# Routed experts in blocks of 32 slots on four column tiles, with down one block behind and ten shared weight places

## What is computed

```python
grp = argmax(xt @ w_rg + b_rg)                      # 4 groups
top_val, top_idx = top_k(in_grp, 2)                 # 2 of the 8 experts of the group
gate = grp_p[:, None] * softmax(top_val)
expert = grp[:, None] * 8 + top_idx                 # 32 experts
# for every token of an expert e:
hid = silu(xb @ w_gate[e]) * (xb @ w_up[e])         # 1024 -> 512
y = hid @ w_down[e]                                 # 512 -> 1024
out[token] += y * gate
```

## Time and profile before

| | |
|---|---|
| median of 3 runs | 2683.63 us |
| the profiled execution's own time | 2685.92 us |
| its span, from the first to the last instruction | 2684.0 us |
| granted TensorE clock, mean | 0.962 |
| first X to last weighing in `experts_stage` | 467.8 to 1079 us |
| bytes moved by DMA | 451.88 MB |
| read from and written to DRAM | 371.86 MB, 58.94 MB |

### The profile page before, as it was taken

One profiled execution on the slowest core, in us unless ns is written; L12 is line 12 of the kernel. 1 busy time (PEld: TensorE's weight loads), 2 busy tenths in 40 slices (PEclk: granted clock), 3 DMA queues, 4 the chain that ended last, 5 costly groups with the idle time before them and its releaser, 6 DMA issues. The chain is left out here.

```text
span 2684.0 us, 39067 instructions
## 1 busy us (share of the span) xinstructions
PE 2437.0 (91%) x14919; PEld 1265.9 (47%) x14919; DVE 1617.9 (60%) x2819; ACT 1082.1 (40%) x1789; POOL 631.3 (24%) x652
## 2 busy tenths in 40 slices
PE   4999895998899999489999999798999999999999
PEld 3555544554455555245434444344454444444544
DVE  7787776222222232557397999844765756747863
ACT  6111454121112122555455648712553634724820
POOL 2012020000000000232244532100630711703602
PEclk8999897999999999789899999899999999999999
DMA  8785758899999999420001329653002002011133
GB/s 246 194 288 170 237 165 283 316 383 387 387 391 366 387 348 332 140 78 32 24 32 56 110 83 184 128 210 126 9 1 102 9 1 102 9 71 40 64 118 126
DMA packets 207372, 451.88 MB, mean 168 GB/s; under 512 B 103600, under 2 KB 113200, under 8 KB 198768
## 3 DMA queue, kind: packets, MB, share of 16 engines
q1 hardware_dynamic: 171344, 368.02, 39.6%
q10 hardware_dynamic: 25696, 48.93, 5.1%
q0 software_dynamic: 10176, 32.78, 4.2%
HBM read 371.86 MB, written 58.94 MB: 161 GB/s over the span
## 5 line engine op out<-in xcount | busy, mean ns | idle before, releaser
L1490 PE MATMUL m_gu<-conv_y,m_xT 128*64 128x256 f32 x1024 | 232.9, 387 | 18.5 <-DMA arena<-in_moe_w_up 16.2
L2728 POOL TENSOR_TENSOR group_words<-group_words 128x1024 f16<-128x1024 f16 x64 | 153.0, 2412 | 377.5 <-PE i_pj L144 368.3
L1492 PE MATMUL m_gu<-arena,m_xT 128*64 128x256 f32 x1024 | 232.9, 387 | 0.0
L1597 DVE TENSOR_TENSOR m_hid<-m_sg,m_gu 64x256 f32<-64x256 f32 x96 | 39.5, 413 | 318.4 <-ACT m_sg L1541 318.4
L1541 ACT ACT_TABLE_LOAD x48 | 61.6, 1283 | 298.1 <-issue 298.1
L1492 PEld LDWEIGHTS m_gu<-arena,m_xT 128*64 128x64 f32 x1024 | 142.7, 140 | 73.8 <-issue 15.4
L1512 PE MATMUL m_y_ps<-arena,m_hidT 128*64 128x512 f32 x768 | 175.4, 598 | 0.0
L1490 PEld LDWEIGHTS m_gu<-conv_y,m_xT 128*64 128x64 f32 x1024 | 142.8, 140 | 36.3 <-issue 25.3
L142 PE MATMUL i_pj<-hT,group_words 128*128 128x512 f16 x384 | 146.5, 381 | 13.1 <-ACT group_words L352 7.7
L142 PE MATMUL s_pj<-hT,arena 128*128 128x512 f16 x368 | 141.9, 386 | 14.1 <-issue 14.0
L143 PE MATMUL i_pj<-hT,group_words 128*128 128x512 f16 x384 | 146.5, 382 | 0.0
(11 more groups left out here) (629 smaller groups left out, 6462.5 us busy)
## 6 DMA issues: line engine op xcount, KB each, us to landing
arena<-in_moe_w_down SPq DMA_DIRECT2D x32, 2048.0 KB, 24.9
conv_y<-in_moe_w_gate SPq DMA_DIRECT2D x22, 2048.0 KB, 17.1
arena<-in_moe_w_up SPq DMA_DIRECT2D x22, 2048.0 KB, 23.9
hT<-in_moe_w_gate SPq DMA_DIRECT2D x10, 2048.0 KB, 16.2
hT<-in_moe_w_up SPq DMA_DIRECT2D x10, 2048.0 KB, 21.9
x_tok<-in_ada_w ACTq DMA_DIRECT2D x8, 2048.0 KB, 12.1
slot_out<-m_y ACTq DMA_DIRECT2D x96, 128.0 KB, 8.0
arena<-in_w_gates SPq DMA_DIRECT2D x23, 512.0 KB, 3.9
```

The lines of the kernel that those rows point to most:

```text
L1490: g = nc.tensor.matmul(gu_ps[i][g_rows, 0:FFN // 2], lhsT=xT[:, c, :], rhs=k.wg[e % WEIGHT_SLOTS][:, c, cols], start=c == 0, stop=c == KC - 1)
L1492: u = nc.tensor.matmul(gu_ps[i][u_rows, 0:FFN // 2], lhsT=xT[:, c, :], rhs=k.wu[e % WEIGHT_SLOTS][:, c, cols], start=c == 0, stop=c == KC - 1)
L1597: nc.vector.tensor_tensor(hid[:, i, :], sg[:, i, :], gu_ps[i][u_rows, 0:FFN // 2], ALU.mult) \
L2728: return tuple(k.nc.gpsimd.tensor_tensor(k.y_U[:, t % 2, n], k.adt_parts[:, n, t, heads].unsqueeze(2).to_broadcast([P, HPG, P]), k.upto16. ...
```

## The change

Blocks have 32 slots instead of 64 and an expert has at least two. The table says for each of 128 partitions which quarter of which token's row it takes: partition 32j+r holds quarter j (256 values, 1 KB) of the row in slot r. With the counts above there are 88 blocks. X is then 2 transposes of 128x128. GU, Y and the table's matmuls use four column tiles of 32 (`tile(j)`): up columns in tiles 0 and 1, gate columns in tiles 2 and 3, and for Y a quarter of the output in each. Each GU tile takes the columns of its weights in neighbouring pairs, with two columns between pairs left to the other tile. Down is loaded as four neighbouring rows a partition. On PE the order becomes X(n+1), GU(n), Y(n-1), H(n). The gain and the shift are one DVE instruction each. The weights have ten places instead of nine (the tenth is half of `x_tok`), shared by all kinds in turn. Gathers go through a ring of four buffers and a POOL copy; stores move from ACT's queue to POOL's, also through a ring of four.

```diff
-BLOCK = P // 2
-SLOT_BLOCKS = 2 * S // BLOCK + EXPERTS
-TABLE_ROWS = SLOT_BLOCKS + 1
+BLOCK, QUARTER = P // 4, D // 4
+RING = 4
+LEAST = 2
+SLOT_BLOCKS = 2 * S // BLOCK + LEAST * EXPERTS
+TABLE_ROWS = SLOT_BLOCKS + 3 * RING
-ZERO_PARTS = 4
+ZERO_PARTS = 6
...
+    spare = k.x_tok[:, TT // 2:TT, :].rearrange("p t d -> p (t d)")
+    k.places = [arena_units(k, n) for n in range(6)] + [halves_of_hT(k, n) for n in range(2)] + [arena_units(k, 6), spare]
...
+def load_unit(k, eng, i):
+    e, part = i // 3, i % 3
+    name = ("moe_w_gate", "moe_w_up", "moe_w_down")[part]
+    source = k.ins[name][turn_of(e)]
+    eng.dma_start(expert_unit(k, e, part), source.rearrange("(p c) n -> p c n", p=P)).then_inc(k.unit_in[i % PLACES], 16)
...
             for n in range(2):
                 for t in range(TT):
-                    last = nc.tensor.matmul(tab_ps[:, :], lhsT=low_hot[:, n, t, :], rhs=blk_hot[:, n, t, :],
...
+                    for j in range(4):
+                        last = nc.tensor.matmul(tab_ps[j * BLOCK:(j + 1) * BLOCK, :], lhsT=low_hot[:, n, t, :],
...
+            def free(i):
+                sp.wait_ge(y_done if i % 3 == 2 else gu_done, 4 * end(sp, i // 3))
+            for i in range(PLACES, UNITS):
+                if (i - PLACES) % 3 != 1:
+                    free(i - PLACES)
+                load_unit(k, sp, i)
...
+            def hand_on(i, n, before):
+                pool.wait_ge(x_in[i], 4 * n - 4 * i + 16)
+                pool.wait_ge(xt_done, before)
+                nc.gpsimd.tensor_copy(xg[:, :], ring[:, i, :]).then_inc(x_copied, 1)
+                pool.wait_ge(x_copied, n + 1)
+                fetch(i, n + RING)
+            def store(i, n):
+                pool.wait_ge(y_read, n + 2)
+                pool.dma_start(k.slot_out[bass.ds(n * BLOCK, BLOCK), :].rearrange("r (j c) -> j r c", j=4),
+                               y[:, i, :]).then_inc(y_stored[i], 16)
+            def give(i, landed):
+                pool.wait_ge(y_stored[i], landed)
+                pool.sem_inc(y_free, 1)
...
+                for c in range(KC):
+                    for j, (part, i) in enumerate(((1, 0), (1, 1), (0, 0), (0, 1))):
+                        last = nc.tensor.matmul(gu_ps[tile(j), 0:FFN // 2], lhsT=xT[:, c % 2, c // 2, :],
+                                                rhs=half_of(expert_unit(k, e, part)[:, c, :], i), start=c == 0, stop=c == KC - 1)
...
                 for c in range(FC):
+                    for j in range(4):
+                        last = nc.tensor.matmul(y_ps[tile(j), 0:QUARTER], lhsT=hidT[:, c, :],
+                                                rhs=expert_unit(k, e, 2)[:, c % 2 * 2 + c // 2, j * QUARTER:(j + 1) * QUARTER],
...
-                with pe.Fori(first, behind) as n:
-                    GU(n, e)
-                    H(n, 0)
-                    X(n + 1)
-                    H(n, 1)
-                    Y(n, e)
+                X(first + 1)
+                wait_unit(k, pe, e, 0)
+                wait_unit(k, pe, e, 1)
+                GU(first, e)
+                if e:
+                    Y(first - 1, e - 1)
+                H(first)
+                with pe.Fori(first + 1, behind) as n:
+                    X(n + 1)
+                    GU(n, e)
+                    Y(n - 1, e)
+                    H(n)
...
+            with dve.Fori(1, blocks) as n:
+                gained(n + 1)
+                dve.wait_ge(gu_done, 4 * n + 4)
+                shifted(n + 1)
+                product_of(n)
+                weigh(n - 1, (n + RING - 1) & (RING - 1))
```

More of the change, by code:

```diff
@@ L1240, in _ @@
             act.wait_ge(gate_mm, 1)
-            for half in range(2):
-                rows_of = slice(half * BLOCK, (half + 1) * BLOCK)
-                nc.scalar.copy(k.gate_half[rows_of, :], gate_ps[rows_of, half * HALF:(half + 1) * HALF])
+            for j in range(4):
+                rows_of = slice(j * BLOCK, (j + 1) * BLOCK)
+                nc.scalar.copy(k.gate_half[rows_of, 0:QUARTER], gate_ps[rows_of, j * QUARTER:(j + 1) * QUARTER])
         @block.vector
@@ L1361, in alloc_expert_weights, with expert_unit, wait_unit @@
 def alloc_expert_weights(k):
[L1363 to L1385, removed]
+    spare = k.x_tok[:, TT // 2:TT, :].rearrange("p t d -> p (t d)")
+    k.places = [arena_units(k, n) for n in range(6)] + [halves_of_hT(k, n) for n in range(2)] + [arena_units(k, 6), spare]
+    k.unit_in = [k.nc.alloc_semaphore(f"m_unit_in{n}") for n in range(PLACES)]
+def expert_unit(k, e, part):
+    n = FFN if part < 2 else D
+    return k.places[(3 * e + part) % PLACES].rearrange("p (c n) -> p c n", n=n)
+def load_unit(k, eng, i):
[3 more added lines that the diff above has]
+    eng.dma_start(expert_unit(k, e, part), source.rearrange("(p c) n -> p c n", p=P)).then_inc(k.unit_in[i % PLACES], 16)
+def wait_unit(k, eng, e, part):
+    i = 3 * e + part
+    eng.wait_ge(k.unit_in[i % PLACES], 16 * (i // PLACES + 1))
 def experts_stage(k):
@@ L1458, in _, with fetch @@
             blocks = end(pool, EXPERTS - 1)
-            def fetch(n, column):
-                nc.gpsimd.tensor_copy(idx[:, :], column).then_inc(idx_ready, 1)
+            rounds = (blocks + RING) >> 2
+            quarters = k.normed_dram.rearrange("s (j d) -> (s j) d", j=4)
+            def fetch(i, n):
+                column = k.slot_token[:, n:n + 1] if isinstance(n, int) else k.slot_token[:, bass.ds(n, 1)]
+                nc.gpsimd.tensor_copy(idx[:, i:i + 1], column).then_inc(idx_ready, 1)
                 pool.wait_ge(idx_ready, n + 1)
@@ L1471, in _ @@
-            with pool.Fori(1, blocks + 1) as n:
-                pool.wait_ge(xt_done, n)
-                fetch(n, k.slot_token[:, bass.ds(n, 1)])
+            for i in range(RING):
+                fetch(i, i)
+            pool.sem_inc(y_free, RING)
+            for i in range(RING):
+                hand_on(i, i, i + 1)
+            for i in range(RING):
+                hand_on(i, RING + i, RING + i + 1)
+                if i >= 2:
+                    give(i - 2, 16)
+                store(i, i)
@@ new lines, in _ @@
+            with pool.Fori(2, rounds) as g:
+                for i in range(RING):
+                    n = g * RING + i
+                    hand_on(i, n, (n <= blocks) * n + (n > blocks) * (blocks + 1) + 1)
+                    give((i + 2) % RING, g * 16 - 16 + 16 * (i // 2))
+                    store(i, n - RING)
+            for i in range(2, RING):
+                give(i, (blocks >> 2) * 16)
+            for i in range(RING):
+                store(i, (blocks >> 2) * RING + i)
+            for i in range(RING):
+                pool.wait_ge(x_in[i], rounds * 16 + 16)
@@ L1967, in _ @@
                     fetch0(t + 6)
+            for i in range(RING):
+                pool.wait_ge(k.y_stored[i], ((blocks + RING) >> 2) * 16)
         @block.vector
@@ L3416, in mixer_program @@
         k.att_stored = nc.alloc_semaphore("att_stored")
[L3417 removed]
+        k.x_natural, k.normed_stored = [nc.alloc_semaphore(f"x_natural{n}") for n in range(2)], [nc.alloc_semaphore(f"normed_stored{n}") for n in range(4)]
         with ExitStack() as first:
```

228 lines of the change are left out of this document (118 added, 110 removed).

## The result

The changed kernel takes 2692.45 us (median of 8 runs, 2687.04 to 2695.17) against 2681.28 us (8 runs) for the kernel before on the same chip: ratio 1.0039, 95% interval 1.0026 to 1.0051. It is slower by 0.4%, where 1.2% faster was forecast. The profiled execution took 2691.96 us, its span is 2690.3 us.

What follows compares the result with a forecast made beforehand. DMA, at 565 us against PE's 504, was to become the expert stage's bound. The stage's end, -38.5 us, and +7 around it gave -31.5 and a forecast of 2652 us, range 2618 to 2700 (8 in 10).

Steps and rivals of the forecast that it cites:

- rival A: GU and Y on PE: only two tiles work at once, a block takes 10.9 us, about 3040 us; chance 0.11.
- PE's block, 5.73 us: PE, one block: GU 3.44, Y 1.72, X, H and tile changes together 0.57 us; 88 blocks are 504 us.
- Rival B: GU's moving operand: column pairs halve the rate, a block takes 9.2 us, time about 2895 us; chance 0.04.
- The ring puts them four blocks (23 us) ahead: POOL's stream: `hand_on` and gather stand behind a `give` waiting for a store, but run four blocks, 23 us, ahead.
- DMA's sum, 565 us: DMA in the expert stage: weights 487 - 5, `x_tok` reload 5.5, gathers and stores 78 us; becomes the bound.
- the 52 ns: Gathers and stores: each 1 KB run takes 52 ns, on a line between 35 ns (512 bytes) and 87 (2 KB).
- rival D: 1 KB runs at 87 ns add 53 us, about 2705; or POOL with its queue exceeds 5.73 us a block; chance 0.06.
- The stage's end, -38.5 us: Expert stage: the last weighing comes at 1040.5 us, against 1078.3 + 0.7 before.
- Around it, +7: Outside the block loop: router +1.4 and +1, first gathers +2.5, next stage's gathers +2, zeroing 0; sum +7 us.
- the stages outside the experts move by more than 7 us: Sign that the forecast is wrong: stages other than the experts shift by over 7 us.
- PE waits for POOL's copies: Sign that the forecast is wrong: PE waits for POOL's copies or for H instead of for weights.
- Rival C: PE issue: record pairs start 0.063 us apart, not 0.054; a block takes 6.6 us, about 2684, no change; chance 0.1.

Runs made afterwards that it cites:

- e6: Changed kernel with down weights back in 4096-byte packets, and gate, up and hidden columns read as neighbours: 2658.04 us.
- e10: Changed kernel with only the down weights back in 4096-byte packets, column pairs kept: 2673.48 us.
- e15: Changed kernel with 4096-byte down packets, neighbouring columns, and stores on ScalarE's queue as four plain transfers a block: 2646.56 us.
- e5: Changed kernel without the four dummy stores and the last two waits for landed stores behind the loop: 2683.91 us.
- e1: Changed kernel with each block's single store issued from ScalarE one block behind, VectorE waiting for landings, no dummy stores: 2749.37 us.
- e16: Changed kernel with its 16384-byte packets and column pairs kept, stores on ScalarE's queue as four plain transfers a block: 2674.57 us.
- e3: Changed kernel with gate's and up's moving operand read as 256 neighbouring columns instead of column pairs: 2689.19 us.
- e2: Kernel before with down as four neighbouring rows a partition, gate and up on column pairs, hidden columns turned to match: 2702.74 us.

## Why the prediction was wrong

- **Four tiles together** (rival A): right; four records within 0.01 us, twice those of the earlier trace rows. The Trainium skill (TensorE: Matmul & The Clock Gate, Part 3: Packing small matmuls) has matmuls in strict order by start and end; a fourth matmul's first record before the first one's second speaks against that, if the two records of one float32 matmul are neighbours in the order.
- **PE's block, 5.73 us**: mis-sized; measured 6.26. H and X together take 0.74 us for 0.57, GU with the pairs 3.68 for 3.44, Y 1.84 for 1.72. With neighbouring columns (e6) a block takes 5.95 (621.03 to 626.98 from X to X). 88 x 6.26 = 551 us is less than the 565 forecast for the DMA, but not less than what the DMA came to (534 us by the bullet on its sum). So with the pairs PE had the larger sum, and that cost: e10, where POOL hardly waits for stores but the pairs are still there, takes 15 us more than e6, and its stage ends 24.9 us sooner than before, not 38.3. This is the second term that failed, about 15 us, beside 19 for the landing.
- **Rival B**, pairs that cost: true, with a factor of 1.06 in place of 2. Priced only as "none" or "double", it left out the size that came. The Trainium skill (SBUF — State Buffer, Specifications (TRN2), on its 16-byte cachelines) would make two accesses to a line free; measured are 0.2275 us for 0.215. (The rival's own sum, 2686 + 807 - 604, is 2889, not 2895.)
- **"The ring puts them four blocks (23 us) ahead"**: the step that failed. The gathers are four ahead, but `hand_on` stands behind a `give`, and this asks for a store issued two blocks, 12.5 us, before; the store's landing was never costed. It is 13.2 us, so each block could wait, and POOL stood in `give` for most of 237 us. The 8.0 us of the kernel before would have fit. What makes the landing late is down's 16 KB packets for the larger part (e10: POOL's waits fall to 9.0 us).
- **DMA's sum, 565 us**: too high for the weights. SP's queue took 0.785 x 615 = 483 us, but for 198.17 MB, with `w_tok` among them: 2.44 us a MB, and 460 us for the forecast's 188.7 MB (89 matrices and half of `x_tok`) in place of 487.5. With 74 us for gathers and stores that makes 534. The -5 us for down's runs was about right (0.799 x 615 / 199.45 = 2.46 us a MB in e6, with 4 KB runs); why the rate is better than the 2.61 of before even there, no run shows. Gathers and stores took 74 us (78), but not by the way that was forecast: on POOL's queue there is no packet of 1 KB.
```profile
DMA packets 32736, 223.48 MB, mean 363 GB/s; under 512 B 13341, under 2 KB 13341, under 8 KB 21314
```
  ScalarE's queue in e15 has such packets, and they bear out the 52 ns: 0.06 x 615 x 16 / 11264 us. So rival D's dear small runs fell. What failed is that "less engine time" was taken for "no later": down's 16 KB runs were booked at -5 us, and cost 19 by the landings of others (e10).
- **The stage's end, -38.5 us**: measured -5.6; with the failed part undone (e6) -38.3. That agreement is luck: the weights were 28 us cheaper than forecast, and against this stand a block of 5.95 for 5.73 us (19 us over 88 blocks), the 5 us that were not there, and engines only 0.77 busy from 471 to 537 us, where the sum took them as full.
- **Around it, +7**: the start came close (first X +3.7 us). The tail was not costed at all: four stores and the waits around them on POOL behind the last block, +13.2 us; e5, without them, gets 8.5 us back. With -5.6 and a small rest this is the 6.3 us by which the span grew. The clause "the stages outside the experts move by more than 7 us" caught it, and "PE waits for POOL's copies" the other.
- **Rival C**, issue at 0.063 us: fell; e6 starts quartets 0.215 us apart, 0.054 us each.

Rival D's second half (POOL with its queue above PE's block) was the nearest, with a chance of 0.06 that it shared. It was dismissed by POOL's own work (2.9 to 4 us a block; 3.3 measured, 633.02 to 636.33), where the question was what POOL waits for. The reading of the slices in the prediction's first lines is off by one and two: the DMA row stands at 9 from the ninth to the sixteenth, which covers the stage to its end.

## What to carry to other kernels

When a wait moves into an in-order stream, write down which event it asks for, how old that event is by then, and the landing time of that transfer under the *new* load. Down in bigger packets was 1% cheaper for SP's queue here (2.44 us a MB for 2.46) and dearer for every small transfer beside it; with small transfers on the path, 4 KB rows beat 16 KB ones by 19 us. Give a transfer to or from 128 partitions a slowest count that is a multiple of 16 (on ScalarE's queue 2647 us with 32, 2733 with 4, 2865 with 2). Two sums within some per cent of each other, 504 and 565 us here, don't yet name the bound: measured they were 551 and 534. And count what is left at a loop's end as part of the change.

## What the runs showed of the hardware

- The landing of small transfers follows the packet size of the other queue (with which the choice of rows changed, too): gathers 12.3 us beside 16384-byte packets only, 6.9 with a third of the bytes in 4096-byte ones (after, e10). Turn-taking between queues would explain it; no row shows a turn. The Trainium skill (DMA: Bandwidth & Descriptors, Queues, rings and completion order) states that each engine goes round the queues packet by packet, which agrees.
- One DMA issue on ScalarE's queue can take 16.2 us instead of 0.55, when its transfer uses 4 engines by its completions (e1); with 16 none took over 1.6 (before, e15, e16). On POOL's queue the same transfer never took over 0.77 us to issue.
- A moving operand of two values in four costs 0.2275 us where neighbours cost 0.215, with four tiles at work (after, e3); with two, GU's groups grow by 16.0 of 348.5 us (e2). A transpose that reads every second column 305 ns for 247 (after, e6):
```profile
L1562 PE MATMUL m_ht<-consts,m_hid 64*128 64x64 f32 x176 | 39.5, 305 | 1.1 <-DVE m_hid L1632 1.1
```
```profile
L1563 PE MATMUL m_ht<-consts,m_hid 64*128 64x64 f32 x176 | 29.3, 247 | 1.1 <-DVE m_hid L1633 1.1
```
- Stays open: why an issue hangs when its transfer uses few engines, and how much of the stores' 13.2 us on POOL's queue is their form and how much their turns.
